# Two transformer blocks on one core: split scores four steps ahead, head turns three steps ahead, and the order of the second block's projections

## The chip, the cores and the metric

One core of one Trainium2 chip runs the whole program. The metric is the device time of one execution in microseconds (us). The engines are TensorE (PE; its weight loads are shown as PEld), VectorE (DVE), ScalarE (ACT), GpSimd (POOL) and SyncE (SP, which issues the loads of the weights).

## The reference

Input x is 512 tokens of 1024 columns. Two layers of a first block are followed by two layers of a second block. The first block has spatial gating, a latent attention of 8 heads (96 columns a head) and a gated linear attention, mixed by sigmoid gates. The change works mostly on the second block, of which one layer is:

```
h = rms_norm(x, norm_g); proj = h @ w_in          # 1024 -> aq ak av ag | bq bk bv bg | mq mg
qa, ka = rope(rms_norm(heads of aq)), rope(rms_norm(heads of ak))       # 6 heads of 64, causal
qb, kb = rope(rms_norm(heads of bq)), rope(rms_norm(heads of bk))       # 6 heads of 64, dilated
mkv = rms_norm(mem) @ w_mem_kv; qm, km = rms_norm(heads)                # 4 heads of 64, 256 memory rows
o = softmax(q @ k.T / 8 + mask) @ v                                     # for each head
x = x + concat(oa * silu(ag), ob * silu(bg), om * silu(mg)) @ w_out
```

All inputs and results are float32. The kernel computes a product of two float32 matrices with three passes of rounded parts: each operand is a high part (type float32r) and a low part (the rest), and the passes are high*high, high*low and low*high, summed in PSUM.

## The kernel before

**Matrix products of the projections.** `plan_groups` (L88) lists the groups of weight columns in the order in which they are used; in the second block mkv, aq, ak, av, bq, bk, bv, mq, ag, bg, mg, out. A group has 8 parts of 128 rows (a step in the ring). SP loads pieces of two parts into `raw`. For each part ACT writes the rounded `w_hi` (`round_weights`, L1036) and DVE writes the rest, `w_lo` (`residue`, L1361), both into a ring of four slots; ACT waits until the part four places back has been used. PE then runs the part's twelve (or nine) passes (`step`, L677, matmuls at L699). A `Splitter` on ACT and one on DVE keep three parts ahead of PE. `evict` and `evict_now` empty the four banks of a group.

**The order of each engine is written out by hand.** `alongside` (DVE) does the split of one part and then so many items of a generator (`per_step`), such as `head_norm` and `rotate`, in which each `yield` ends an item. `head_squares` on ACT makes the squares whose sums `head_norm` takes.

**Attention as a stream.** `Stream` makes units (a pair of heads g and a block i of 128 queries; a causal unit has i+1 key blocks, a memory unit two) and steps (at most two key blocks of a unit). In the second block there are 8 pairs, 32 units and 44 steps in a layer. Each engine walks the same steps. PE in step n: the events of `begin[n]`, a share of the remaining projections as filler (`fill`; bv, mq, ag, bg, mg and five parts of out), the product with v of the pair before (`values`, L795) in a pair's first step, and the transposes of the step's probabilities (`turn_probs`, L783). The events are `turn` (transposes of q and k of a pair of heads, L754), `scores` (L766) and, on DVE, `scale`. The chain of a unit is: scores on PE, mask and row maximum on DVE (L1522), Exp on ACT (L1091), reciprocal and scale on DVE (L1530, L1534), transposes on PE, copy on ACT (L1105), product with v.

**What sets the order before.** Scores of a unit stand two steps ahead of its first step. Probabilities have three buffers. The turn of a pair stands one to five steps ahead of its first scores. Scores of two heads are two float32 matmuls of 128 rows: `kT_2` holds each head's keys with zeros in the other head's half (POOL writes the zeros once), so DVE makes three copies for each turn (L1502, and L1506 twice). Scores and turns share the two PSUM banks `S_BANKS`. A score needs its bank read by whoever had it last. On ACT and DVE a step's `split_beside` moves the weight splits on: on ACT ahead of the step's other work, on DVE after `begin[n]` and ahead of `extra(n)`.

**Evictions.** DVE empties ak, bq, bv and mq; ACT empties aq, av, bk and the gates (with Silu).

## Time and profile before

| | |
|---|---|
| median of 3 runs | 1673.48 us (1673.45 to 1674.01) |
| the profiled execution's own time | 1672.92 us |
| span of its instructions | 1671.1 us |
| busy shares of the span | PE 96%, PEld 79%, DVE 59%, ACT 44%, POOL 3% |
| first layer of block 2, attention | about 1121 to 1321 us of the span |
| second layer of block 2, attention | about 1437 to 1640 us |

Busy time is the union of the instructions of an engine. A matmul's end is modelled, so successive passes overlap in the profile: what one costs PE is the distance from its start to the next start. "Idle" is the time in which nothing of the engine runs, and a releaser is the instruction that ended it. A float32 matmul is two records in the profile, a float32r pass one. "Granted clock" is the share of TensorE's full clock.

### The profile page before, as it was taken

To read this page: it belongs to the slowest core of one execution; us is meant where nothing else is said; L and a number is where in the kernel's file an instruction comes from. 1 tells how busy PE (TensorE), PEld (TensorE's weight loads), DVE (VectorE), ACT (ScalarE), POOL (GpSimd) and SP (SyncE) were. 2 spreads that over 40 slices of the span, in tenths; PEclk is the share of its full clock that TensorE was granted. 3 is DMA by queue.
4 is the path that set the end of the run, shared out by engine and by line. 5 is a ranking of instruction groups with operands and counts; after the bars stand their busy time and mean duration, and the time that the engine had idled before them with its cause. 6 is when DMAs were issued, how large, how long until landed. Compare 5 with 4: busy or idle time off the path is not lost.

```text
span 1671.1 us, 21692 instructions
## 1 busy us (share of the span) xinstructions
PE 1601.1 (96%) x8121; PEld 1317.0 (79%) x8121; DVE 993.0 (59%) x2214; ACT 730.1 (44%) x1503; POOL 48.1 (3%) x76
## 2 busy tenths in 40 slices
PE   6999999999999999999999999999989999998999
PEld 6887778788887887777788887998766789975677
DVE  4597655444344488756443445487876555688663
ACT  4444444333233443543433334435456554344662
POOL 0000001000001000001000001000000010000000
PEclk9999999999999999999999999999999999999999
DMA  7332122333333332112333232331112223211121
GB/s 221 88 88 75 51 64 64 101 89 89 102 98 95 93 90 76 51 51 77 88 89 101 89 126 82 104 86 54 57 29 73 91 87 95 79 51 42 35 76 63
DMA packets 80884, 136.24 MB, mean 82 GB/s; under 512 B 8190, under 2 KB 33420, under 8 KB 80780
## 3 DMA queue, kind: packets, MB, share of 16 engines
q1 hardware_dynamic: 77264, 129.48, 26.0%
q10 hardware_dynamic: 3516, 5.37, 1.0%
q8 instruction: 65, 1.06, 0.3%
q14 instruction: 39, 0.32, 0.1%
HBM read 132.74 MB, written 2.10 MB: 81 GB/s over the span
## 4 chain that ended last, share of the span: by engine, by line
PE 75%; DVE 17%; ACT 5%; issue 2%; DMA 0%; ACTq 0%; POOL 0%; DVEq 0%
PE gemm_bank L699 61%; PE aux_bank L766 4%; PE aux_bank L795 3%; DVE w_lo L1367 3%; PE aux_bank L783 3%; DVE rope L1466 2%; ACT w_hi L1044 1%; PE aux_bank L754 1%; DVE head_sums L1419 1%; DVE probs L1522 1%; ACT probs L1091 1%; DVE kT L1506 1%; DVE probs L1534 1%; PE aux_bank L671 1%; PE aux_bank L730 1%
## 5 line engine op out<-in xcount | busy, mean ns | idle before, releaser
L1044 ACT ACTIVATE w_hi<-raw 128x512 fp32r<-128x512 f32 (+3 forms) x524 | 305.6, 587 | 669.6 <-PE gemm_bank L699 668.2
L1367 DVE TENSOR_TENSOR w_lo<-raw,w_hi 128x512 fp32r<-128x512 f32 (+3 forms) x524 | 330.3, 636 | 442.6 <-ACT w_hi L1044 441.0
L699 PE MATMUL gemm_bank<-act_hi,w_hi 128*128 128x512 f32 x768 | 316.5, 412 | 7.9 <-DVE mq_flat L1407 3.8
L699 PE MATMUL gemm_bank<-act_hi,w_lo 128*128 128x512 f32 x768 | 300.4, 391 | 0.0
L699 PE MATMUL gemm_bank<-act_lo,w_hi 128*128 128x512 f32 x768 | 299.8, 390 | 0.0
L699 PE MATMUL gemm_bank<-w_hi,act_hi 128*128 128x384 f32 (+3 forms) x736 | 269.6, 366 | 6.1 <-DVE bq L1407 2.9
L699 PE MATMUL gemm_bank<-w_lo,act_hi 128*128 128x384 f32 (+3 forms) x736 | 257.6, 350 | 0.0
L699 PE MATMUL gemm_bank<-w_hi,act_lo 128*128 128x384 f32 (+3 forms) x736 | 257.4, 350 | 0.0
L699 PEld LDWEIGHTS gemm_bank<-act_hi,w_hi 128*128 128x128 f32 x768 | 144.7, 188 | 43.8 <-issue 11.2
L699 PEld LDWEIGHTS gemm_bank<-act_lo,w_hi 128*128 128x128 f32 x768 | 144.8, 189 | 31.8 <-issue 2.9
L699 PEld LDWEIGHTS gemm_bank<-act_hi,w_lo 128*128 128x128 f32 x768 | 144.4, 188 | 31.0
L699 PEld LDWEIGHTS gemm_bank<-w_hi,act_hi 128*128 128x128 f32 x736 | 139.4, 189 | 23.9 <-issue 9.7
L699 PEld LDWEIGHTS gemm_bank<-w_lo,act_hi 128*128 128x128 f32 x736 | 139.4, 189 | 11.3 <-issue 1.9
L699 PEld LDWEIGHTS gemm_bank<-w_hi,act_lo 128*128 128x128 f32 x736 | 139.1, 189 | 9.7
L766 PE MATMUL aux_bank<-kT,qT 128*128 128x256 f32 (+7 forms) x384 | 121.6, 435 | 5.9 <-DVE kT L1506 4.8
L1105 ACT ACTIVATE probsT<-aux_bank 128x256 f32<-128x256 f32 (+1 forms) x136 | 71.8, 528 | 114.3 <-PE aux_bank L783 113.5
L1091 ACT ACTIVATE probs<-probs,neg_max 128x128 f32<-128x128 f32 (+2 forms) x192 | 104.2, 544 | 35.6 <-DVE neg_max L1522 35.2
L783 PE MATMUL aux_bank<-ident,probs 128*128 128x128 f32 x464 | 75.7, 279 | 14.4 <-DVE probs L1534 14.2
L766 PEld LDWEIGHTS aux_bank<-kT,qT 128*128 128x128 f32 (+1 forms) x384 | 64.2, 193 | 27.5 <-DVE kT L1506 9.2
L783 PEld LDWEIGHTS aux_bank<-ident,probs 128*128 128x128 f32 x464 | 56.3, 141 | 37.0 <-DVE probs L1534 21.0
L699 PE MATMUL gemm_bank<-y_hi,w_hi 128*128 128x512 f32 x192 | 74.8, 390 | 0.3 <-ACT gate L1225 0.3
L699 PE MATMUL gemm_bank<-y_hi,w_lo 128*128 128x512 f32 x192 | 74.7, 389 | 0.0
(287 smaller groups left out, 2087.9 us busy)
## 6 DMA issues: line engine op xcount, KB each, us to landing
raw<-in_w_in SPq DMA_DIRECT2D x104, 512.0 KB, 3.6
raw<-in_w_in SPq DMA_DIRECT2D x64, 384.0 KB, 3.3
raw<-in_w_out SPq DMA_DIRECT2D x32, 512.0 KB, 3.7
raw<-in_w_branch SPq DMA_DIRECT2D x24, 512.0 KB, 3.7
raw<-in_w_mem_kv SPq DMA_DIRECT2D x8, 512.0 KB, 3.6
raw<-in_w_in SPq DMA_DIRECT2D x16, 256.0 KB, 2.8
raw<-in_w_in SPq DMA_DIRECT2D x8, 416.0 KB, 4.7
x<-in_x SPq DMA_DIRECT2D x4, 512.0 KB, 5.2
```

What stands on the lines that cost most here:

```text
L671: last = pe.transpose(bank[0:rows, t * P:(t + 1) * P], source(t, kk), ident[:, :])
L699: last = pe.matmul(o, a, c, start=begin and n == 0, stop=end and n == 2)
L730: last = pe.transpose(bank[:, t * P:(t + 1) * P], source[:, t, kk * P:(kk + 1) * P], ident[:, :])
L754: last = pe.transpose(bank[0:kind.rows, t * P:(t + 1) * P], of(h, t), ident[:, :])
L766: pe.matmul(bank[:, 0:n_keys * P], a.qT_of(g, x)[:, i * P:(i + 1) * P], a.kT_of(g, x)[:, 0:n_keys * P], start=True, stop=True).then_inc(fu ...
L783: last = pe.transpose(bank[:, c:c + P], probs[a.where][m % 3][:, x, j * P:(j + 1) * P], ident[:, :])
L795: last = pe.matmul(bank[x * HD:(x + 1) * HD, kind.first_i(j) * P:T], kind.v_of(a.head(g, x), j), a.probsT_of(g, x, j), start=(j == 0), sto ...
L1044: act.activation(w_hi[:, s % RING, 0:n], raw[:, p % RAW, kk % PIECE, 0:n], ACT.Copy)\
L1091: act.activation(rows, rows, ACT.Exp, bias=neg_max[:, c:c + 1], scale=-1.0, accum_out=row_sum[:, c:c + 1]).then_inc(probs_ready, 1)
L1105: act.activation(a.turned_to(m, j0, j1), bank[:, 0:2 * (j1 - j0) * P].rearrange("p (x j s) -> p x j s", x=2, s=P), ACT.Copy)\
L1367: dve.tensor_tensor(w_lo[:, s % RING, 0:n], raw[:, p % RAW, kk % PIECE, 0:n], w_hi[:, s % RING, 0:n].bitcast(F32), ALU.subtract).then_inc( ...
L1466: mark(dve.tensor_tensor(tmp[i][:, :, :, :], xx, t4, ALU.mult))
```

## The change

In the second block:

- The keys and queries turned by PE are split like weights: ACT writes the high parts (`turned_hi`), DVE, one step later, the low parts (event `low`). Scores are three float32r passes of 64 rows, head 0 in rows 0 to 63 and head 1 in rows 64 to 127, alternating (`scores_2`). The zeroed keys and their memset go.
- Scores stand up to four steps ahead, with four buffers of probabilities. `together` computes units 0 and 1 of a causal pair into one bank with one hand-over, and memory units two by two. Turns stand three steps ahead of their pair's first scores (two for pair 1, two for pair 7).
- av is projected last of the six, so that the first turn lies in av and not in bk; bq, bv and mq are emptied by ACT; the b heads' norm and rotation start beside av.
- On DVE a step's extra work comes ahead of its weight splits, and `rotate` yields after each instruction. In the first block DVE takes three items, not two, in each part of u and za.

The diff, cut to its core:

```diff
@@ -136,9 +136,9 @@
         two("mkv", 0, 2 * WE, NMEM // P, "w_mem_kv_2")
         two("aq", 0, WA)
         two("ak", WA, WA)
-        two("av", 2 * WA, WA)
         two("bq", 4 * WA, WB)
         two("bk", 4 * WA + WB, WB)
+        two("av", 2 * WA, WA)
         two("bv", 4 * WA + 2 * WB, WB)
         two("mq", 4 * WA + 4 * WB, WE)
         two("ag", 3 * WA, WA, WA // P)
...
@@ -526,11 +528,23 @@
                 self.steps += mine
             self.lead, self.middle = {}, {}
             self.begin = [[] for _ in self.steps]
+            self.turns, self.buffers = [], len(probs[self.where])
             for m, mine in enumerate(self.steps_of):
                 self.begin[mine[0]].insert(0, ("scale", m))
-                if mine[0] >= 2:
-                    self.begin[mine[0] - 2].append(("scores", m))
+                if mine[0] >= 2 and self.together(m):
+                    last = max(self.together(m)) - self.buffers
+                    free = self.steps_of[last][-1] + 1 if last >= 0 else 0
+                    self.begin[max(mine[0] - SCORES_LEAD[block], free, 0)].append(("scores", m))
             self.fill(fill, weight)
+        def together(self, m):
+            if self.block == 1:
+                return {m: 0}
+            kind, i = self.kind(m), m % NT
+            if kind.name == "memory":
+                return {} if i % 2 else {m: 0, m + 1: kind.n_keys(i) * P}
+            return {0: {m: 0, m + 1: P}, 1: {}}.get(i, {m: 0})
 
...
             self.begin[step].append(("turn", g, x))
+            if self.block == 2:
+                at = [event[0] for event in self.begin[step + 1]].index("scores") \
+                    if "scores" in [event[0] for event in self.begin[step + 1]] else len(self.begin[step + 1])
+                self.begin[step + 1].insert(at, ("low", g, x))
 
         def head(self, g, x):
...
                    DEPTH * UNITS_1 + l * UNITS_2, fill, lambda n: 1.3 if n < 13 else 0.9)
-        a.lead = {4: [("turn", 0, 0)], 5: [("scores", 0)], 6: [("scores", 1)]}
-        for g, (at_pair, step) in {1: (0, 1), 2: (0, 3), 3: (2, 1), 4: (2, 3), 5: (3, 3), 6: (4, 3), 7: (5, 3)}.items():
+        a.lead = {3: [("turn", 0, 0)], 4: [("low", 0, 0)], 5: [("scores", 0)]}
+        for g, (at_pair, step) in {1: (0, 0), 2: (0, 5), 3: (1, 5), 4: (2, 5), 5: (3, 5), 6: (4, 5), 7: (5, 4)}.items():
             a.turn_at(g, 0, a.first_step_of(at_pair) + step)
+        a.turns = list(range(len(a.pairs)))
         return a
 
...
 
+        def scores_2(a, m):
+            g, kind = m // NT, a.kind(m)
+            if m % NT == 0:
+                aux_wait_read(pe, a.key("q", g, 0))
+                aux_wait_read(pe, a.key("k", g, 0))
+            banks = [aux_open(a.key("S", m, x), S_BANKS[x]) for x in range(2)]
+            for mm, c in a.together(m).items():
+                i, keys = mm % NT, kind.n_keys(mm % NT) * P
+                for n, (qq, kk) in enumerate(((q_hi, k_hi), (q_lo, k_hi), (q_hi, k_lo))):
+                    for x in range(2):
+                        r = slice(x * HD, (x + 1) * HD)
+                        last = pe.matmul(banks[x][:, c:c + keys], qq[r, g % 2, i * P:(i + 1) * P],
+                                         kk[r, g % 2, 0:keys], start=n == 0, stop=n == 2)
+                        if n == 2 and mm == max(a.together(m)):
+                            last.then_inc(full_of(a.key("S", m, x)), 1)
         def begin(a, what, *of):
             if what == "turn":
                 turn(a, *of)
...
@@ -974,10 +1017,10 @@
 
         def block_2(l):
             gemm(gi_of(2, l, "aq"), "tokens", ready=part_ready((2, l, "x")))
-            for name in ("ak", "av", "bq"):
+            for name in ("ak", "bq", "bk"):
                 gemm(gi_of(2, l, name), "tokens")
             a = attention_2(l)
-            gemm_led(gi_of(2, l, "bk"), "tokens", a, lambda kk: None)
+            gemm_led(gi_of(2, l, "av"), "tokens", a, lambda kk: None)
             y_ready = lambda kk: pe.wait_ge(y2_lo_ready, KD * l + kk + 1)
             attention(a, y_ready)
...
                 wait_gemm_full(act, gi, b)
                 act.activation(dst(b), gemm_bank[b][:, 0:groups[gi].n], func).then_inc(gemm_read[b], 1)
 
+        def turned_hi(a, g):
+            for what, hi in (("q", q_hi), ("k", k_hi)):
+                bank = aux_wait_full(act, a.key(what, g, 0))
+                n = T if what == "q" else a.pairs[g][0].k_tiles * P
+                act.activation(hi[:, g % 2, 0:n], bank[:, 0:n], ACT.Copy).then_inc(turned_hi_ready, 1)
         def exponentials(a, m):
-            kind, i = a.kind(m), m % NT
-            keys = kind.n_keys(i) * P
-            for x in range(2):
-                c = a.column(m) + x
-                aux_wait_read(act, a.key("S", m, x))
-                rows = probs[a.where][m % 3][:, x, 0:keys]
-                act.activation(rows, rows, ACT.Exp, bias=neg_max[:, c:c + 1], scale=-1.0,
-                               accum_out=row_sum[:, c:c + 1]).then_inc(probs_ready, 1)
+            for mm in a.together(m):
+                for x in range(2):
...
             for n, (m, j0, j1) in enumerate(a.steps):
                 split_beside(split, a, n, evict_beside)
+                for event in a.begin[n] if a.block == 2 else ():
+                    if event[0] == "turn":
+                        turned_hi(a, event[1])
                 for event in a.begin[n] + a.middle.get(n, []):
                     if event[0] == "scores":
...
             for n, _ in enumerate(head_squares(kind_tiles("a"), sq_2)):
-                split.beside(gi_of(2, l, "av"), n // 2)
-            evict(gi_of(2, l, "av"), ACT.Copy, lambda b: flat_2("av")[:, b, :])
-            split.through(gi_of(2, l, "bq"))
-            a = attention_2(l)
-            gi = gi_of(2, l, "bk")
-            split.beside(gi, 5)
-            exponentials(a, 0)
-            split.beside(gi, 6)
-            exponentials(a, 1)
-            evict(gi, ACT.Copy, lambda b: flat_2("bk")[:, b, :])
+                split.beside(gi_of(2, l, "bq"), n // 2)
+            for name in ("bq", "bk"):
+                evict(gi_of(2, l, name), ACT.Copy, lambda b: flat_2(name)[:, b, :])
             wait_gemm_read(act, gi_of(2, l, "bq"))
             wait_gemm_read(act, gi_of(2, l, "bk"))
             b_squares = head_squares(kind_tiles("b"), sq_2)
+            a = attention_2(l)
+            gi = gi_of(2, l, "av")
+            for kk in range(KD):
+                for _ in range(2):
+                    next(b_squares, None)
+                split.beside(gi, kk)
+                if kk == 3:
+                    turned_hi(a, 0)
+                if kk == 6:
+                    exponentials(a, 0)
+            evict(gi, ACT.Copy, lambda b: flat_2("av")[:, b, :])
             m_squares = head_squares([mq_tok[:, t, :, :] for t in range(NT)]
...
             for i, xx in enumerate((x1, x2, x1, x2)):
                 t4 = table[:, i, :, :].unsqueeze(2).to_broadcast([P, NT, heads, half])
                 mark(dve.tensor_tensor(tmp[i][:, :, :, :], xx, t4, ALU.mult))
-                if i % 2:
-                    yield
+                yield
             settle()
             mark(dve.tensor_tensor(x1, tmp[0][:, :, :, :], tmp[1][:, :, :, :], ALU.subtract))
+            yield
             mark(dve.tensor_tensor(x2, tmp[2][:, :, :, :], tmp[3][:, :, :, :], ALU.add))
             yield
 
...
                 scaled(a, *of)
 
         def turned(a, g, x):
-            kind = a.pairs[g][0]
-            bank = aux_wait_full(dve, a.key("q", g, x))
-            dve.tensor_copy(a.qT_of(g, x), bank[0:kind.rows, :]).then_inc(read_of(a.key("q", g, x)), 1)
-            bank = aux_wait_full(dve, a.key("k", g, x))
-            for hh in range(kind.group):
-                r = slice(hh * kind.d, (hh + 1) * kind.d)
-                ins = dve.tensor_copy(a.kT_of(g, x + hh)[r, 0:kind.k_tiles * P], bank[r, 0:kind.k_tiles * P])
-                if hh == kind.group - 1:
-                    ins.then_inc(read_of(a.key("k", g, x)), 1)
-                else:
-                    mark(ins)
+            if a.block == 1:
+                bank = aux_wait_full(dve, a.key("q", g, x))
+                dve.tensor_copy(a.qT_of(g, x), bank[0:QK, :]).then_inc(read_of(a.key("q", g, x)), 1)
+                bank = aux_wait_full(dve, a.key("k", g, x))
+                dve.tensor_copy(a.kT_of(g, x), bank[0:QK, :]).then_inc(read_of(a.key("k", g, x)), 1)
+                return
+            for n, (what, hi, lo) in enumerate((("q", q_hi, q_lo), ("k", k_hi, k_lo))):
+                key = a.key(what, g, 0)
+                columns = T if what == "q" else a.pairs[g][0].k_tiles * P
+                dve.wait_ge(turned_hi_ready, 2 * a.turn_count(g) - 1 + n)
+                dve.tensor_tensor(lo[:, g % 2, 0:columns], aux_bank[aux_place[key][0]][:, 0:columns],
+                                  hi[:, g % 2, 0:columns].bitcast(F32), ALU.subtract).then_inc(read_of(key), 1)
 
         def scores(a, m):
 
-            kind, i = a.kind(m), m % NT
-            keys = kind.n_keys(i) * P
-            if m >= 3:
-                aux_wait_full(dve, a.key("T", a.steps_of[m - 3][-1]))
+            kind, units = a.kind(m), a.together(m)
+            if max(units) >= a.buffers:
+                aux_wait_full(dve, a.key("T", a.steps_of[max(units) - a.buffers][-1]))
             for x in range(2):
-                c = a.column(m) + x
                 key = a.key("S", m, x)
                 bank = aux_wait_full(dve, key)
-                dve.tensor_tensor_reduce(out=probs[a.where][m % 3][:, x, 0:keys], in0=bank[:, 0:keys],
-                                         in1=kind.mask(i), scale=-kind.scale, scalar=3.0e38, op0=ALU.add, op1=ALU.min,
-                                         accum_out=neg_max[:, c:c + 1]).then_inc(read_of(key), 1)
+                for mm, b in units.items():
+                    c, keys = a.column(mm) + x, kind.n_keys(mm % NT) * P
+                    ins = dve.tensor_tensor_reduce(out=probs[a.where][mm % a.buffers][:, x, 0:keys],
+                                                   in0=bank[:, b:b + keys], in1=kind.mask(mm % NT), scale=-kind.scale,
+                                                   scalar=3.0e38, op0=ALU.add, op1=ALU.min,
+                                                   accum_out=neg_max[:, c:c + 1])
+                    if mm == max(units):
+                        ins.then_inc(read_of(key), 1)
+                    else:
+                        mark(ins)
 
...
                 for event in a.begin[n] + a.middle.get(n, []):
                     if drain and event[0] == "turn":
                         drain(event[1])
-                    begin(a, *event)
+                    else:
+                        begin(a, *event)
+                extra(n)
                 split_beside(split, a, n, evict_beside)
-                extra(n)
                 g = m // NT
                 if g and n == a.first_step_of(g):
                     evicted_out(a, g - 1, evict_out)
...
 
             a = attention_1(l)
             work = prepare()
-            alongside(work, [gi_of(1, l, n) for n in ("u", "za")], 2, at_end, False)
+            alongside(work, [gi_of(1, l, n) for n in ("u", "za")], 3, at_end, False)
 
             def sum_out(g):
...
+            alongside(a_heads, [gi_of(2, l, n) for n in ("bq", "bk")], 2)
             for kk in range(KD):
                 for event in a.lead.get(kk, []):
-                    begin(a, *event)
-                split.beside(gi_of(2, l, "bk"), kk)
+                    if event[0] != "turn":
+                        begin(a, *event)
+                for _ in range(2):
+                    next(b_heads, None)
+                split.beside(gi_of(2, l, "av"), kk)
 
             def drain(g):
                 for _ in b_heads if g == FIRST_B else m_heads if g == FIRST_M else ():
```

## Rows read from the trace of the kernel before

**Rows 1.** The page: busy time by engine, and the chain by engine.

```profile
PE 1601.1 (96%) x8121; PEld 1317.0 (79%) x8121; DVE 993.0 (59%) x2214; ACT 730.1 (44%) x1503; POOL 48.1 (3%) x76
...
PE 75%; DVE 17%; ACT 5%; issue 2%; DMA 0%; ACTq 0%; POOL 0%; DVEq 0%
```

**Rows 2.** Busy time in both attentions of block 2: PE, PEld, DVE, ACT, POOL, clock.

```profile
1121.30:1321.60 200.30, 187.34 (x1005) 146.08 (x1005) 139.01 (x409) 106.57 (x264) 0.00 (x0) 0.99 0.18 56
1436.80:1640.50 203.70, 188.89 (x1005) 147.19 (x1005) 139.38 (x409) 105.48 (x263) 0.00 (x0) 0.98 0.18 55
```

**Rows 3.** PE's waits, 1121 to 1321.5; last row 1436.7 to 1640.5: total, times, longest.

```profile
PE aux_bank L783 <- DVE probs L1534: 6.0, 5, 2.0
PE aux_bank L766 <- DVE kT L1506: 2.4, 5, 0.8
PE aux_bank L795 <- ACT probsT L1105: 1.5, 1, 1.5
PE gemm_bank L699 <- DVE bq L1407: 1.4, 1, 1.4
PE gemm_bank L699 <- DVE mq_flat L1407: 1.1, 1, 1.1
PE gemm_bank L699 <- DVE bv L1407: 0.8, 1, 0.8
PE aux_bank L766 <- DVE qT L1502: 0.5, 1, 0.5
...
PE gemm_bank L699 <- DVE mq_flat L1407: 2.7, 1, 2.7
```

**Rows 4.** The chain in order of time: start, us, what, count.

```profile
245.09 19.27 PE gemm_bank L699 x84
...
1052.75 31.22 PE gemm_bank L699 x180
...
1176.25 1.72 PE aux_bank L766 x4
```

**Rows 5.** Timeline of PE, 256-column passes after scores: start, duration.

```profile
1177.92 0.28 PE L699 MATMUL gemm_bank<-w_lo,act_hi 128*128 128x256 f32 x1
1178.04 0.28 PE L699 MATMUL gemm_bank<-w_hi,act_lo 128*128 128x256 f32 x1
```

**Rows 6.** Timeline of PE in the linear attention of block 1.

```profile
264.19 1.03 PE L671 MATMUL aux_bank<-ident,qk_c 128*128 128x128 f32 x8
265.16 2.27 PE L925 MATMUL aux_bank<-qk_c,kt_dn 64*128 64x128 f32 x32
267.36 1.13 PE L940 MATMUL aux_bank<-vc,ks_tok 64*64 64x128 f32 x16
```

**Rows 7.** DVE by line and shape, 1045 to 1361: busy us, mean ns.

```profile
L1367 DVE TENSOR_TENSOR w_lo<-raw,w_hi 128x512 fp32r<-128x512 f32 x24 | 16.1, 689 | 14.6 <-ACT w_hi L1044 14.6
...
L1506 DVE COPY kT<-aux_bank 64x512 f32<-64x512 f32 x12 | 8.2, 684 | 0.2
...
L1522 DVE CUSTOM_DVE_ANT_0 probs<-aux_bank,mask_causal 128x384 f32<-128x384 f32 x6 | 3.2, 553 | 1.0 <-PE aux_bank L766 1.0
...
L1534 DVE TENSOR_SCALAR probs<-probs,row_inv 128x128 f32<-128x128 f32 x12 | 2.9, 284 | 0.2
```

**Rows 8.** ACT by line and shape, the same stretch.

```profile
L1105 ACT ACTIVATE probsT<-aux_bank 128x512 f32<-128x512 f32 x32 | 18.8, 588 | 16.8 <-PE aux_bank L783 16.5
L1044 ACT ACTIVATE w_hi<-raw 128x512 fp32r<-128x512 f32 x24 | 14.4, 625 | 9.1 <-PE gemm_bank L699 9.1
```

**Rows 9.** PE by stretch, before and after its longest wait: busy, granted clock.

```profile
1185.00:1188.00 3.00, 1.25 (x11) 1.00 0.03 10
1188.00:1192.00 4.00, 3.91 (x16) 0.57 0.30 98
```

**Rows 10.** PE's waits in block 1's first layer, 60 to 165.

```profile
PE aux_bank L754 <- DVEq L1476: 1.6, 1, 1.6
PE gemm_bank L699 <- DVE w_lo L1367: 1.0, 2, 0.7
```

62 lines of the change are left out of this document (32 added, 30 removed).

## The prediction

> **What bounds the kernel now.** I read the page first: PE is busy for 96% of the span and holds 75% of the chain [rows 1], so time comes mainly from less PE work or fewer PE waits. The stretches of the two attentions of block 2 come next [rows 2]: 200.3 and 203.7 us, with PE busy for 187 and 189, DVE 139, ACT 106. No engine but PE is near its bound over the whole of a stretch, so what PE waits for there is order and latency. Third, PE's waits in that stretch [rows 3]: 14.1 us of idle time in 16 waits, most of it for scaled probabilities (6.0), turned keys and queries (2.4 + 0.5), and evictions by DVE (bq 1.4, mq 1.1, bv 0.8). The second layer has the same rows except mq, 2.7; with it 16.0 us. A wait costs a little more than its idle time, because a modelled end covers part of the next start: from the starts in the timeline I take 0.2 us more each. That makes 17.3 + 19.2 = 36.5 us of waits in both layers that this change could touch.
>
> **PE's work in the scores.** Before: four records of 512 columns (both heads) take 1.72 us [rows 4], so a block of 128 keys for both heads costs 0.43. A causal pair has 10 blocks, 4.30 us; a memory pair 8, 3.44. After: a float32r pass has a start-to-start distance of 19.27/84 = 0.229 us at 512 columns and 31.22/180 = 0.173 at 384 [rows 4], and 0.12 at 256 [rows 5]. The trace has no float32r pass of 128 columns and none on half the rows. For the half rows the nearest rows are those of the linear attention [rows 6]: 32 records of 64 rows, alternating halves and banks, take 2.20 us (265.16 to 267.36), where 8 records of 128 rows take 0.97, 0.12 each. At 0.12 each one after the other they would take 3.9. So both halves work at the same time; two side by side cost 0.11 to 0.14. I take 0.11 for a pair of 128-column passes, and what 16 x 0.11 = 1.8 leaves of 2.2, 0.2 for each of its two batches, as the price of changing over to half rows. A causal pair then costs 3 x (0.11 + 0.12 + 0.173 + 0.229) = 1.90 plus three batches x 0.2, 2.5 us: 1.8 less. A memory pair costs 4 x 3 x 0.12 = 1.44 plus two batches, 1.84: 1.6 less. Six and two pairs give 14.0 us a layer, **28.0 in both**. Bounds: with no price for changing over, 22 batches x 0.2 x 2 = 9 more is gained; if the passes of the two heads add up, 4.4 and 3.28 us a pair, nothing is gained (28 worse). If a 128-column pass costs what float32 does (0.21), 3 x 0.1 x 6 x 2 = 3.6 comes back.
>
> The Trainium skill speaks against the half rows: "TensorEngine Tiling (Array Packing)", Key Properties, says that changing the tiling mode drains TensorE. The row gives 0.2 us for a batch, on entry. If leaving cost as much again, 44 x 0.2 = 9 us would come back and the sum below would be 1648.
>
> **Waits that go.** Scores four steps ahead, with the mask, Exp and scale of a unit two steps further from its transposes, cover the waits for probabilities. ACT empties bq, bv and mq bank by bank (0.49 us for 384 columns by the rows of other evictions) while PE works on; PE's next group then finds bank 0 free. The waits for probabilities, bq, bv and mq go: 9.3 us idle in layer one, 10.9 in two, with 9 x 0.2 each 23.8 together. The cover is DVE's: beside av it has 16 items of b_heads, eight weight parts, a low pair and the first masks, some 17 us against 18.3 of PE; in steps 0 to 5 some 24 against 22. So DVE is the later one there, and I leave 1.5 us a layer for it. The 2.05 us of three copies a turn (0.69 + 2 x 0.68) [rows 7] become two low parts on DVE (1.38) and two high parts on ACT (0.59 each, from a copy out of PSUM) [rows 8]; ACT gains some 16 us a layer on 106 and is no bound.
>
> **Waits that come.** Turn and scores share two banks. Turns 2 to 6 are transposed in a pair's last step n, the low part is made at the start of n+1, and scores of another unit follow there at once; they need both banks read. ACT comes to the high part only after its weight split, which waits for PE's last part but one. From that moment: w_hi 0.63 [rows 8], w_lo 0.69 [rows 7], scale of a 128-key unit 0.16 + 2 x 0.28, low q and low k 0.69 each, and semaphores 0.3, about 3.4 us; PE has 0.9 to 1.8 us of filler and transposes left (step 11 has ACT's eviction of mq in the way as well, 1.5 us). By the filler of each step I get waits of 2.0, 2.0, 0.4, 2.2 and 2.5 us: 9.1 a layer, in place of 2.9 idle and 1.2 of restarts before. In step 0 scores of unit 2, scores of unit 3 and turn 1 follow each other through the same two banks. Behind each stand PE's latency of 0.35, two masks (2 x 0.55 at 384 columns, and 2 x 0.69 at 512, which is what every DVE operation of 512 columns takes) [rows 7] and 0.3 of semaphores, less the batch's own 0.5 to 0.7: 1.5 and 1.9, 3.4 us that did not exist. What stands behind these waits is PE's filler, no more.
>
> Sum for both layers: before 36.5; after 2 x (9.1 + 3.4 + 1.5) = 28.0, plus 4.6 for the waits of `values` and of the gate bg, which stay: 32.6. **3.9 us less.**
>
> **Block 1.** PE waits 1.6 us for the heads at its first turn and 1.0 for weight parts [rows 10]; the second layer has the same two. DVE's timeline shows hardly a gap from 97 us to that turn, at 139. At three items a part, the heads are done before u is multiplied by za (2.4 us), so the 1.6 goes and the waits for weight parts stay or grow a little. I take 1.5 a layer, 3.0; bounds 2 us worse (parts late) and 5 better.
>
> **Hidden or nothing.** POOL's memset, the order of av (its product comes 12 us later), a fourth probability buffer: PE has waits on none of them in [rows 3]. SP's loads follow the same ring; av's only change place. I take 0 us, with one either way.
>
> **The sum** is made against the profiled execution's 1672.9 us, 0.6 under the median of the runs: 1672.9 - 28.0 - 3.9 - 3.0 = 1638.0, in terms of the median **1638.6**.
>
> **Rivals.**
>
> *Heads one after the other.* The passes of the two halves add up: nothing of the 28.0 is gained, 1667. Against it are the 2.20 us of [rows 6]; for it, that these are float32 records and not float32r. 7%.
>
> *Few new waits.* The turns' waits stay at what they are before (4.1 a layer, not 9.1) and step 0's halve, since ACT reaches the high parts earlier than I reckon: 2 x (5.0 + 1.7) = 13.4 less, 1625. For it: step 18's is only 0.4 by the same working. 25%.
>
> *The clock.* After a wait of 1.84 us the granted clock is 0.57 over 4 us, part full and part at 1.2 GHz instead of 2.4, which costs 4 x 0.43 = 1.7 us [rows 9]; each layer has one such stretch. If all seven new waits are followed by one, 14 x 1.7 = 24 less the 3.4 of before: 1659. Against it: the longest wait of that layer, 2.0 us [rows 3], is followed by none. 9%. (The Trainium skill, "TensorE: Matmul & The Clock Gate", part 1, says idle time sends the clock to half; the row agrees, 0.57 after 1.84 us.)
>
> *Weight parts late, slower than before.* DVE now takes its scores, which wait for PE's, and two items before a step's weight split. Once DVE is more than the ring's three parts behind (about 6 us of PE's filler), PE waits for w_lo in every step. From 35/88 = 0.4 us a step on, over 88 steps, the gain is gone; at 0.5 it is 1683. For it: DVE's share in steps 0 to 18 is near PE's. Against it: PE's waits for w_lo in the attentions before are nil in [rows 3] though DVE was as busy. 6%.
>
> **Chances.** The forecast has 53%. The range that should hold 8 in 10 goes from 1614 (few new waits and no changeover price) to 1662 (clock, or most of the half-row gain lost). About 0.2%, 3.3 us, is what a measurement of this kernel can tell from no change. Faster by more: 0.91; within: 0.03; slower: 0.06.
>
> **What would show it.** Right: scores of 512 keys, both heads, take about 0.7 us of PE instead of 1.72, with starts of the two halves a few ns apart; no PE wait for probabilities, bq, bv, mq; a new PE wait for k_lo of about 9 us a layer in five places, and for the masks in step 0. Wrong: equal distances between all six passes of a unit (heads in turn), PE waits for w_lo above 2 us a layer, clock stretches after each k_lo wait, or k_lo waits under 4 us a layer.

## The result and the profile after

The changed kernel takes 1676.9 us where the kernel before takes 1673.6 in the same comparison (20 runs each): ratio 1.0022, 95% interval 1.0014 to 1.0029. It is 3.4 us slower by the medians, 0.2%, and not 35 us faster. One of the six runs of a_two below took 2207.3 us at a granted clock of 0.68, in a slow state: without it the median is 1663.1, with it the 1663.9 that the expectations name. The profiled execution has a span of 1673.4 us, 2.3 more than the one before. Its page answers to [rows 1]:

```profile
PE 1589.0 (95%) x8249; PEld 1307.8 (78%) x8249; DVE 969.8 (58%) x2174; ACT 750.1 (45%) x1559; POOL 46.4 (3%) x75
...
PE 83%; DVE 10%; ACT 5%; issue 2%; DMA 0%; ACTq 0%; POOL 0%; DVEq 0%
```

PE is busy for 12 us less in a span that is 2 us longer, so some of the saving is there, and more idle time (14 us) stands against it. The page does not say where.

The first view to read is one row for each stage, from the transposes of x_n of a block to those of the next. Columns: stretch, length, then busy time with the number of instructions of PE, PEld, DVE, ACT and POOL, granted clock, DMA share, GB/s. Before:

```profile
12.00:523.40 511.40, 501.10 (x2457) 410.23 (x2457) 286.57 (x570) 207.34 (x386) 16.45 (x20) 1.00 0.30 87
523.40:1043.60 520.20, 507.87 (x2497) 413.97 (x2497) 292.27 (x572) 214.82 (x401) 22.37 (x29) 1.00 0.29 86
1043.60:1359.20 315.60, 299.32 (x1606) 248.83 (x1605) 211.44 (x547) 158.17 (x371) 5.56 (x14) 0.99 0.24 71
1359.20:1668.00 308.80, 292.37 (x1565) 243.80 (x1563) 200.66 (x527) 142.90 (x335) 0.00 (x0) 0.99 0.22 66
```

After:

```profile
12.50:530.80 518.30, 503.38 (x2456) 410.11 (x2457) 286.54 (x570) 206.61 (x385) 16.45 (x20) 0.99 0.30 86
530.80:1058.90 528.10, 513.48 (x2497) 417.56 (x2498) 292.60 (x572) 214.89 (x401) 20.55 (x28) 0.98 0.29 85
1058.90:1370.10 311.20, 290.46 (x1670) 243.73 (x1669) 199.68 (x527) 168.25 (x399) 5.56 (x14) 0.98 0.24 72
1370.10:1670.20 300.10, 281.25 (x1629) 236.18 (x1627) 188.82 (x506) 153.21 (x363) 0.00 (x0) 0.98 0.23 68
```

Two things cancel. Block 1, the first two rows, is longer by 6.9 + 7.9 = 14.8 us, though PE's work in it is the same. Block 2 is shorter by 4.4 + 8.7 = 13.1 us, well short of the 31.9 forecast for it. The granted clock is lower in all four rows. Before, the trace has 4 stretches at half clock (1.2 GHz instead of 2.4) of 3.4 us each, one of them in block 1. After, it has 11 of about 3.4 us and two of 6.8, five of them in block 1 (23.9 us), seven in block 2 (23.9 us) and one at the very end.

PE's waits in both attentions of block 2, first layer and second (total, times, longest), are the rows that answer to [rows 3]:

```profile
PE aux_bank L807 <- DVE k_lo L1571: 8.6, 5, 2.0
PE aux_bank L826 <- DVE probs L1601: 5.1, 4, 2.4
PE aux_bank L826 <- ACT probsT L1160: 1.7, 2, 1.2
PE aux_bank L807 <- DVE neg_max L1584: 1.6, 1, 1.6
PE gemm_bank L721 <- ACT bgT L1380: 1.1, 1, 1.1
PE aux_bank L776 <- DVE neg_max L1584: 0.8, 1, 0.8
...
PE aux_bank L807 <- DVE k_lo L1571: 7.4, 4, 2.0
PE aux_bank L826 <- DVE probs L1601: 5.4, 4, 2.4
PE aux_bank L826 <- ACT probsT L1160: 2.8, 3, 1.2
```

The waits for bq, bv and mq are gone and those for k_lo have come, as forecast. The waits for scaled probabilities (L826 for probs) have stayed: 5.1 and 5.4 us, 6.0 before. The idle time is 18.9 and 18.7 us in place of 14.1 and 16.0.

In block 1, PE's waits from 60 to 165 us, to be held against [rows 10]:

```profile
PE gemm_bank L721 <- DVE w_lo L1428: 7.6, 4, 3.6
PE gemm_bank L721 <- DVE c_lo L1455: 0.9, 1, 0.9
```

The wait for the heads at the first turn (1.6) is gone, as intended, and weight parts cost 7.6 in its place. DVE's timeline shows why (start, duration, what, count; idle time before it and its releaser in brackets):

```profile
80.40 0.68 DVE L1428 TENSOR_TENSOR w_lo<-raw,w_hi 128x512 fp32r<-128x512 f32 x1
81.00 2.46 DVE L1715 BATCH_NORM_STATS2 stats<-vn 128x6 f32<-128x512 f32 x4
...
86.34 0.68 DVE L1428 TENSOR_TENSOR w_lo<-raw,w_hi 128x512 fp32r<-128x512 f32 x1
87.96 1.81 DVE L1480 TENSOR_REDUCE head_sums<-sq 128x8 f32<-128x768 f32 x2 [0.93 <-ACT sq L1107]
90.68 0.95 DVE L1480 TENSOR_REDUCE head_sums<-sq 128x8 f32<-128x768 f32 x1 [0.91 <-ACT sq L1107]
91.55 0.68 DVE L1428 TENSOR_TENSOR w_lo<-raw,w_hi 128x512 fp32r<-128x512 f32 x1
...
95.12 0.68 DVE L1428 TENSOR_TENSOR w_lo<-raw,w_hi 128x512 fp32r<-128x512 f32 x1
...
101.70 0.69 DVE L1428 TENSOR_TENSOR w_lo<-raw,w_hi 128x512 fp32r<-128x512 f32 x1
```

These five weight parts start 5.3 us apart on average (21.3 / 4), where PE works one off in 12 x 0.229 = 2.7. The items between them are the dear ones: statistics of 2.5 us, sums of 768 columns of 0.95 each that also wait for ACT's squares, and a chain of twelve small steps for the roots. With three of them a part, DVE uses up its lead over PE, and PE has to wait. Three of its four waits fall here (0.4, 0.5 and the first line below). The fourth comes later in the same way: the weight parts at 111.53 and 117.68 stand 6.2 us apart, with two products of 2.5 us between them.

```profile
102.44 0.79 PE L721 MATMUL gemm_bank<-act_hi,w_hi 128*128 128x512 f32 x1 [3.57 <-DVE w_lo L1428]
...
118.42 0.50 PE L721 MATMUL gemm_bank<-act_hi,w_hi 128*128 128x512 f32 x1 [3.13 <-DVE w_lo L1428]
```

The scores themselves overlap as forecast, but take longer: 512 keys of both heads 1.09 us, where the sign of being right was 0.7. Timeline of PE, one unit of 384 keys, both heads; `64*128` with x2 is one pass of each head:

```profile
1173.15 0.38 PE L826 MATMUL aux_bank<-ident,probs 128*128 128x128 f32 x2
1173.46 0.44 PE L807 MATMUL aux_bank<-k_hi,q_hi 64*128 64x384 f32 x2
1173.74 0.34 PE L807 MATMUL aux_bank<-k_hi,q_lo 64*128 64x384 f32 x2
1173.91 0.33 PE L807 MATMUL aux_bank<-k_lo,q_hi 64*128 64x384 f32 x2
1174.18 0.44 PE L721 MATMUL gemm_bank<-w_hi,act_hi 128*128 128x384 f32 x1
1174.46 0.34 PE L721 MATMUL gemm_bank<-w_lo,act_hi 128*128 128x384 f32 x1
```

The recorded starts of the two heads are 3 ns apart: both work at once. But something stands at either end of the batch. The two transposes end their share at 1173.37 (1173.15 + 2 x 0.11), the second gemm pass starts at 1174.46, and the first one's share is 0.17: the batch took 1174.29 - 1173.37 = 0.92 us, and its passes are 3 x 0.173 = 0.52. The other 0.40 stands half before the first and second pass of the batch and half before the first and second pass behind it, on full rows.

### The profile page after: what moved, and what is told of

Same layout as the page of the kernel before. It is cut to its first block, busy times and chain, and to the rows that moved or that the text cites. A ratio compares the mean times of both kernels' runs of the same rounds, so it can differ in the third digit from the quotient of the medians.

```text
span 1673.4 us, 21983 instructions
## 1 busy us (share of the span) xinstructions
PE 1589.0 (95%) x8249; PEld 1307.8 (78%) x8249; DVE 969.8 (58%) x2174; ACT 750.1 (45%) x1559; POOL 46.4 (3%) x75
## 4 chain that ended last, share of the span: by engine, by line
PE 83%; DVE 10%; ACT 5%; issue 2%; DMA 0%; ACTq 0%; POOL 0%; DVEq 0%
PE gemm_bank L721 69%; PE aux_bank L838 3%; PE aux_bank L826 3%; PE aux_bank L807 2%; PE aux_bank L791 2%; DVE w_lo L1428 2%; PE aux_bank L776 1%; ACT probs L1143 1%; ACT w_hi L1087 1%; DVE probs L1601 1%; DVE probs L1584 1%; DVE head_sums L1480 1%; PE aux_bank L693 1%; PE aux_bank L752 1%; PE aux_bank L997 0%
## 5 line engine op out<-in xcount | busy, mean ns | idle before, releaser
L721 PE MATMUL gemm_bank<-act_lo,w_hi 128*128 128x512 f32 x768 | 304.2, 396 | 0.0
L721 PE MATMUL gemm_bank<-act_hi,w_lo 128*128 128x512 f32 x768 | 304.1, 396 | 0.0
L826 PE MATMUL aux_bank<-ident,probs 128*128 128x128 f32 x464 | 75.2, 278 | 15.5 <-DVE probs L1601 10.6
L826 PEld LDWEIGHTS aux_bank<-ident,probs 128*128 128x128 f32 x464 | 55.9, 141 | 38.6 <-DVE probs L1601 16.5
L721 PE MATMUL gemm_bank<-y_lo,w_hi 128*128 128x512 f32 x192 | 74.7, 389 | 0.0
L1601 DVE TENSOR_SCALAR probs<-probs,row_inv 128x128 f32<-128x128 f32 (+2 forms) x192 | 64.5, 378 | 3.4
```

Of the source, the lines that this page charges most:

```text
L721: last = pe.matmul(o, a, c, start=begin and n == 0, stop=end and n == 2)
L826: last = pe.transpose(bank[:, c:c + P], probs[a.where][m % a.buffers][:, x, j * P:(j + 1) * P], ident[:, :])
L1601: ins = dve.tensor_scalar(rows, rows, row_inv[:, c + x:c + x + 1], None, ALU.mult)
```

## Experiments

Each was timed in rounds with the kernel before, and the ratio is to that one. "Stages" are the four of the first view.

| run | edit | us | ratio, 95% |
|---|---|---|---|
| change | | 1676.9 | 1.0022 [1.0014, 1.0029] |
| a_two | two items a part in block 1 | 1663.1 | 0.9935 [0.9919, 0.9950] |
| b_three | before, with three items | 1692.4 | 1.0108 [1.0092, 1.0123] |
| c_low | a_two, low parts in the turn's step | 1648.1 | 0.9843 [0.9828, 0.9858] |
| d_mlater | a_two, memory items a step later | 1659.4 | 0.9904 [0.9886, 0.9921] |
| e_both | c_low and d_mlater | 1636.9 | 0.9783 [0.9771, 0.9796] |
| f_split_first | a_two, extra items behind the split | 1677.9 | 1.0026 [1.0017, 1.0036] |
| g_heads_in_turn | a_two, passes of one head, then the other | 1664.4 | 0.9949 [0.9937, 0.9961] |
| h_lead_two | a_two, scores two steps ahead | 1665.4 | 0.9950 [0.9936, 0.9964] |
| i_before_halves | before, float32 scores on half rows | 1662.1 | 0.9932 [0.9919, 0.9944] |
| j_plain | e_both, float32 scores on half rows | 1635.0 | 0.9769 [0.9755, 0.9782] |
| l_uza | e_both, u times za later | 1629.3 | 0.9738 [0.9725, 0.9751] |
| m_single | l_uza, one unit a batch | 1635.8 | 0.9768 [0.9755, 0.9782] |
| k_plain_uza | j_plain and l_uza | 1628.6 | 0.9729 [0.9716, 0.9742] |

**a_two and b_three: the number of items.**

```
-            alongside(work, [gi_of(1, l, n) for n in ("u", "za")], 3, at_end, False)
+            alongside(work, [gi_of(1, l, n) for n in ("u", "za")], 2, at_end, False)
```

> The changed kernel with one edit taken back: in the first block DVE takes two items, not three, in each part of u and za. Theory (three items a part starve PE of weight parts): PE's waits for w_lo before the first turn fall from 7.6 and 6.8 us in the two layers to about 1.5 each, the half-clock stretches of 3.4 us there (2 and 3) go, and the time falls by about 14 us, to 1663. Rival (the first block lost its time through the single-instruction items of rotate, or through extra work ahead of the splits in its attention): the waits for w_lo stay near 7 us and the time stays at 1675 to 1677.

> The kernel before with that edit alone: three items a part in u and za. Theory: it alone costs what the first block lost, 12 to 15 us, 1686 to 1688, with 6 to 8 us of PE waits for w_lo in each layer. Rival (it needs the finer items of rotate to do harm): 1672 to 1676.

a_two: 14 us less than the change, with stages of 513.2, 521.3, 311.3 and 300.0: what the stages give, 11.9, is all from block 1. PE's waits there, with two items:

```profile
PE aux_bank L776 <- DVEq L1537: 3.8, 1, 3.8
PE gemm_bank L721 <- DVE c_lo L1455: 0.9, 1, 0.9
PE gemm_bank L721 <- DVE w_lo L1428: 0.3, 1, 0.3
```

The wait at the first turn, 1.6 before the change, is 3.8 here, and block 1 is still 2.9 us longer than before. In the timeline the four products of a rotation now fill two weight parts instead of one, since `rotate` yields after each instruction, and so the heads are done later.

b_three is the same edit put into the kernel before: 18 us more, and block 1 longer by 19.2 (521.5 and 529.3). PE's wait for weight parts from 60 to 165 us:

```profile
PE gemm_bank L699 <- DVE w_lo L1367: 7.2, 5, 3.5
```

So the third item alone makes the loss in block 1, and does so without the rest of the change. The rest of the change is worth 1 - 0.9935, 11 us.

**c_low: the low parts.** ACT makes the high parts ahead of its weight split, and DVE the low parts in the turn's own step instead of the next.

```
             for n, (m, j0, j1) in enumerate(a.steps):
-                split_beside(split, a, n, evict_beside)
                 for event in a.begin[n] if a.block == 2 else ():
                     if event[0] == "turn":
                         turned_hi(a, event[1])
+                split_beside(split, a, n, evict_beside)
...
-                    else:
+                    elif event[0] != "low":
                         begin(a, *event)
                 extra(n)
+                for event in a.begin[n] if a.block == 2 else ():
+                    if event[0] == "turn":
+                        turned(a, *event[1:])
                 split_beside(split, a, n, evict_beside)
```

> As a_two, and in the second block ACT writes the high parts of a turn ahead of its weight split, and DVE the low parts in the step of the turn, after the extra work and ahead of its split, not at the start of the next step. Theory (PE waits for k_lo because both engines reach the parts only after a weight split that itself waits for PE): the waits for k_lo fall from 8.6 us in five places to under 1.5 a layer, some of the half-clock stretches behind them go, and the time falls by 15 to 22 us against a_two, to about 1644. Rival (DVE is the bound there, and what it does earlier it lacks later): the wait turns up as a wait for probabilities or masks, and the time is within 6 us of a_two.

15 us less than a_two. The waits for k_lo fall from 8.6 and 7.4 to 0.7 and 1.5, those for probabilities stay (5.2 and 5.3). The stages of block 2 are 16.9 us shorter: their idle time falls from 39.6 to 27.2, and their half-clock stretches go from 7 to 4, 1.7 us each. Block 1, which the edit does not touch, is 2.7 us longer, with four such stretches for three.

**d_mlater: the memory heads' sums.** After step n's transposes ACT makes squares for the memory heads, and DVE adds them up within its extra items. In the changed kernel these stand ahead of the weight split and the next scale, and wait for the squares. DVE's waits from 1205 to 1234 us in the changed kernel:

```profile
DVE head_sums L1480 <- ACT sq L1107: 9.0, 3, 4.9
```

Two of the three in its timeline:

```profile
1217.08 0.74 DVE L1480 TENSOR_REDUCE head_sums<-sq 128x4 f32<-128x256 f32 x2 [4.93 <-ACT sq L1107]
1217.74 0.55 DVE L1428 TENSOR_TENSOR w_lo<-raw,w_hi 128x384 fp32r<-128x384 f32 x1
1218.21 0.68 DVE L2028 COPY ya_T<-aux_bank 128x512 f32<-128x512 f32 x1
1218.81 0.15 DVE L1597 RECIPROCAL row_inv<-row_sum 128x2 f32<-128x2 f32 x1
1219.00 0.62 DVE L1601 TENSOR_SCALAR probs<-probs,row_inv 128x256 f32<-128x256 f32 x2
1221.30 0.74 DVE L1480 TENSOR_REDUCE head_sums<-sq 128x4 f32<-128x256 f32 x2 [1.69 <-ACT sq L1107]
```

PE had been waiting for that scale and came to its transposes at once behind it:

```profile
1219.67 0.66 PE L826 MATMUL aux_bank<-ident,probs 128*128 128x128 f32 x4 [1.95 <-DVE probs L1601]
```

```
-                for work in [b_heads] + [m_heads] * (n > n_m):
+                for work in [b_heads] + [m_heads] * (n > n_m + 1):
```

> As a_two, and DVE starts the norm of the memory heads one step later (step 13, not 12). Theory (DVE's extra work now stands ahead of its split and of the next step's scale, and its sums wait for squares that ACT makes only after PE's transposes of the same step: 9.0 us of DVE idle in three waits between 1205 and 1234): those waits go, PE's waits for probabilities fall from 5.1 us to about 1.5 a layer, and the time falls by 7 to 11 us against a_two, to about 1654. Rival (these waits come from DVE's load in steps 12 to 18): no change against a_two, within 2 us.

The waits for probabilities fall from 5.1 and 5.4 to 1.1 and 1.1, as expected, so their cause is shown. The time falls by 3.7 us only, where 7 to 11 were expected: the waits for k_lo rise to 10.3 in both layers, and the first layer (311.0) is no shorter at all, with 20.5 us at half clock in place of 13.7.

**e_both.**

> The changed kernel with two heads' items a weight part in block 1, the low parts of a turn made in the turn's own step, and the memory heads' items one step later. Theory (the waits for k_lo and those for scaled probabilities are separate and add): from the run with early low parts (1648.1) the probability waits fall from 5.2 and 5.3 us to about 1.1 a layer, 8 to 9 us less, k_lo stays under 2 a layer: 1639.5. Rival 1 (clock): what the waits give is taken by half-clock stretches that fall elsewhere, as in the first layer of the run with later items: 1644. Rival 2 (the same delay seen twice): with DVE's later items the low parts come late again, k_lo back at 5 or more a layer: 1648.

26 us less than a_two, where the two edits by themselves gave 15 and 3.7. In the stages of block 2 it is 25.6, and by themselves 16.9 and 6.7, so they add there, and a little more. One part of the theory fails: the waits for k_lo are 3.2 in both layers, not under 2, and above the 0.7 and 1.5 of c_low. The later items still push the low parts back, by less than rival 2 had it. The waits for probabilities are 1.1 and 1.1.

**f_split_first: the order on DVE.**

```
+                split_beside(split, a, n, evict_beside)
                 extra(n)
-                split_beside(split, a, n, evict_beside)
```

> The changed kernel with two items a part, and DVE's extra items of a step behind the step's weight part again, as before the change. Theory (the sums of the memory heads wait on DVE for ACT's squares, and scales and weight parts stand behind them): the weight part no longer stands behind the sums but the next step's scale still does: probability waits 5.1 to about 3 a layer, 4 us less in all than with two items: 1660. Rival (the place of the items in the step is what makes the waits): both waits of 2 us vanish, 8 less: 1656. Rival (nothing): 1664, waits as before. Block 1 stays within 2 us.

Both the theory and its rivals fall: it is 15 us slower than a_two. Waits for k_lo go from 8.6 and 7.4 to 11.0 and 9.8, those for probabilities from 5.1 and 5.4 to 6.5 and 7.1, and block 2 has 37.5 us at half clock in place of 23.9. By the order of the program the extra items, sums included, then stand right ahead of the next step's scale and low parts; that this is the cause was not tested by itself. The extra items hurt in either place, and "ahead of the weight part" is the better one; with the rest of the change, that part of it is a gain.

**g_heads_in_turn: do the halves need each other as neighbours?** The x loop is put outside the three passes.

> The changed kernel with two items a part; the three passes of a unit's scores are issued for one head and then for the other, not alternately. Theory (passes on different halves of the rows run side by side only when they are neighbours in the order): of six passes two neighbours still overlap, the others add up: a causal pair 1.58 us more, a memory pair about 1.2, 6 x 1.6 + 2 x 1.2 = 12 us a layer less the overlap across units: 19 us more than 1663.9, 1683. Rival (no overlap worth having, all six add up and did so already): 1664. Rival (nothing overlaps when in turn): 28 more, 1692. In the timeline the starts of one head's passes are a full pass apart.

No difference beyond the intervals. One rival had the time, but for a reason that the trace denies: there is an overlap. In this kernel the program says q_hi, q_lo, k_lo of head 0, then the same of head 1; the timeline shows the pairs of both heads side by side all the same, with starts 10 to 41 ns apart:

```profile
1171.47 0.50 PE L807 MATMUL aux_bank<-k_hi,q_hi 64*128 64x512 f32 x2 [1.95 <-DVE k_lo L1571]
1171.78 0.43 PE L807 MATMUL aux_bank<-k_hi,q_lo 64*128 64x512 f32 x2
1172.01 0.58 PE L807 MATMUL aux_bank<-k_lo,q_hi 64*128 64x512 f32 x2
```

Each half takes its own passes in order and does not wait for the other's.

**h_lead_two: is the lead of four steps worth anything?** `SCORES_LEAD` of block 2 is 2.

> The changed kernel with two items a part and the scores of block 2 two steps ahead as before the change, not four. Theory (the lead of four hides the way from the mask to the scaled probability; the waits of 2 us come from the memory sums and are there with either lead): waits for probabilities rise from 5.1 to about 9 a layer, waits for k_lo fall from 8.6 and 7.4 to about 4, since the scores stand further behind the turn: 1663, within 4 of 1663.9. Rival (the lead brings the gain): k_lo waits stay, probabilities 6 a layer worse: 1676. Rival (the lead is harmful): waits for probabilities stay at 5, k_lo falls to 3: 1654.

The intervals overlap; waits for probabilities 4.5 and 4.9, for k_lo 9.1 and 8.0. The time follows the theory, but not its working: neither wait moved by more than 0.6. The lead brings nothing in this kernel, where PE waits for a scale that is late behind the sums (d_mlater). Whether it brings something once those waits are gone, as in e_both, was not run.

**i_before_halves: the saving of the halves by itself.** In the kernel before, one kT without zeros, and

```
-                pe.matmul(bank[:, 0:n_keys * P], a.qT_of(g, x)[:, i * P:(i + 1) * P],
-                          a.kT_of(g, x)[:, 0:n_keys * P], start=True, stop=True).then_inc(full_of(key), 1)
+                r = slice(x * HD, (x + 1) * HD) if kind.group == 2 else slice(0, kind.rows)
+                pe.matmul(bank[:, 0:n_keys * P], a.qT_of(g, x)[r, i * P:(i + 1) * P],
+                          a.kT_of(g, x)[r, 0:n_keys * P], start=True, stop=True).then_inc(full_of(key), 1)
```

> The kernel before with one thing changed: the scores of block 2 are plain float32 products on half the rows, one head on each half, from one kT without zeros; everything else, order and leads too, as before. Theory (the halves work side by side whatever their order, also in float32): a causal pair 4.30 becomes 2.15 plus 0.2 for each of four batches, a memory pair 3.44 becomes 1.72 plus 0.8, 6 x 1.35 + 2 x 0.92 = 9.9 us a layer, 20 in both; one copy of 0.69 less a turn, 2 us of kT waits less in both layers: 1652. Rival (the overlap belongs to float32r): nothing from PE, 1672. Rival (the saving of the halves is taken back by waits for probabilities, since PE comes to them earlier): 1660.

11.4 us, not 21. Float32 passes do run side by side, so that rival is out. The rival at 1660 has nearly the time, but not the cause: the waits for probabilities are 5.8 in both layers, where they were 6.0 and 6.2. The timeline of a 512-key batch, kernel before and then this one:

```profile
1175.65 0.60 PE L783 MATMUL aux_bank<-ident,probs 128*128 128x128 f32 x4
1176.09 1.88 PE L766 MATMUL aux_bank<-kT,qT 128*128 128x512 f32 x4
1177.40 0.69 PE L699 MATMUL gemm_bank<-w_hi,act_hi 128*128 128x256 f32 x1
```

```profile
1174.62 0.60 PE L784 MATMUL aux_bank<-ident,probs 128*128 128x128 f32 x4
1175.15 1.13 PE L767 MATMUL aux_bank<-kT,qT 64*128 64x512 f32 x4
1176.21 0.39 PE L699 MATMUL gemm_bank<-w_hi,act_hi 128*128 128x256 f32 x1
1176.43 0.28 PE L699 MATMUL gemm_bank<-w_lo,act_hi 128*128 128x256 f32 x1
```

Before, the second gemm pass starts at 1177.92 [rows 5], and less one pass of 0.12 the batch ends at 1177.80: 1.72 us after the transposes. On half rows it is from 1175.06 to 1176.31, 1.25 us, where half of 1.72 is 0.86. The same reckoning gives 0.62, 0.83 and 1.04 at 128, 256 and 384 columns: always 0.40 above half (0.22, 0.43 and 0.65). A layer then saves 32.9 - 29.1 = 3.8 us, 7.6 in both; PE's waits give another 3.3 (26.8 in place of 30.1). That is 10.9 of the 11.4.

**j_plain: three float32r passes or one float32 pass.** q and k are copied by DVE alone, and ACT makes no high parts.

> The kernel with two items, early low parts and later memory items, but with plain float32 scores on the halves in place of three float32r passes: no high and low parts of q and k, two copies a turn on DVE, none on ACT. Theory (one float32 pass costs 0.86 at 512 columns where three float32r passes cost 0.69, 2 us a layer more; the k_lo waits of 3.2 a layer go, since DVE needs no ACT): 1636.9 + 4 - 6 = 1635, within 4 of 1636.9. Rival (the three passes are worth more than that, as in the width of the change itself): 1645. Rival (ACT's high parts held up its weight parts too): 1629.

The time is the theory's, 1635.0, but by luck: the waits that were to go did not. Batches are 1.06 to 1.27 us in place of 0.92 to 1.17, and the waits for k_lo of 3.2 become waits for kT of 3.1 a layer, so it was DVE's order that made those, not ACT; what became less is a wait for bgT (1.8 to 1.1) and for mq_flat (1.0 to nothing). In block 2 there are also two half-clock stretches fewer (one for three). Dearer passes against fewer waits and stretches: the split of q and k into parts is worth nothing that can be measured here.

**l_uza: work of DVE ahead of the first turn of block 1.**

```
-            alongside(work, [gi_of(1, l, n) for n in ("u", "za")], 2, at_end, False)
+            alongside(work, [gi_of(1, l, n) for n in ("u", "za")], 2, None, False)
...
                 split.beside(gi_of(1, l, "zb"), kk)
+                if kk == 5:
+                    at_end(gi_of(1, l, "za"))
```

> The kernel with two items, early low parts and later memory items, and in block 1 u times za moved from the end of za to behind the first turn beside zb. Theory (DVE has no gap for 45 us before the first turn of block 1 and the wait of 3.8 us there is for its heads, so every us of other work moved behind it comes off the wait): 2.49 us less a layer, 5 in both: 1632. The wait for DVEq at the turn 3.8 becomes 1.3. Rival (the product then stands ahead of a weight part or of the sums and makes a new wait there): 1637.

The wait at the turn is 1.4 (3.8 before the edit), as expected, and the time 7.5 us less, not 5. The idle time of block 1 is 5.4 less, and the half-clock stretches behind that wait (at 140 and 652 us in e_both) are gone too; one new stretch has come at 524 us.

**m_single and k_plain_uza.** `together(m)` returns `{m: 0}` in m_single, so each layer has 32 units in batches of their own, and the scores and Exp of unit 1 get their own place beside av.

> The kernel with u times za moved (1629.3), in which each unit's scores stand alone: 32 batches a layer in place of 21, same passes, same columns, same order otherwise. Theory (each batch on half rows costs 0.40 us beside its passes, about half going in and half coming out, as the starts around a batch show): 11 x 0.40 x 2 = 8.8 us more, 1638. Rival (only the way in costs, 0.2, as the prediction had it): 1633.7. Rival (a batch costs nothing by itself, the 0.4 are waits of the masks): 1629.

> The two edits that were best by themselves put together: plain float32 scores on the halves (1635.0) and u times za behind the first turn (7.5 less than 1636.9). Theory (they touch different stretches and add): 1627.5. Rival (the float32 passes cost 2 us a layer more PE time than float32r, and their gain was in waits that the other has no more): 1631.

m_single is 6.5 us slower than l_uza (5.0 by the ratios). A batch of 128 and 256 columns took 1.09 us; alone they take 0.68 and 0.75. Two of 256 took 1.11; alone 0.75 each. So an extra batch costs 0.34 to 0.39 us, 6 x 0.34 + 4 x 0.39 = 3.6 a layer, 7.2 in both, and the stages of block 2 are 5.9 us longer. There were 22 batches a layer before the edit, not the 21 of the expectation, so 10 more and not 11: at 0.40 each that makes 8.0. The price is one of each batch, in and out; "only the way in" would be 4.0, and the ratios alone would not exclude it, but the rows do. k_plain_uza is the fastest of all, 45 us faster than the kernel before, though not by more than its interval than l_uza.

## Why the prediction was wrong

- **PE's work in the scores: size off.** Six pairs of 4.3 and two of 3.5 were 32.9 us a layer before, as reckoned. After, batches of 1.09, 0.92 and 1.15 make 3.16 a causal pair, and two of 1.11 a memory pair: 6 x 3.16 + 2 x 2.22 = 23.4. The saving is 9.5 a layer, **19.0 in both and not 28.0**. The step that failed is "I take ... 0.2 for each of its two batches": it read the way in and left out the way out. [rows 6] could not show that one: behind the 32 records come more passes on 64 rows. The prediction had the other end in hand, in the sentence on the Trainium skill, "TensorEngine Tiling (Array Packing)", Key Properties, whose drain at a change of mode it priced at 9 us. The trace agrees with that rule: 0.40 us around each batch. But that all of it is the drain isn't shown: in [rows 6] the second batch too begins dearer (the starts around its first passes are 0.22 and 0.18 us apart, the others 0.11), though the passes right before it are on 64 rows as well. The rival "heads one after other" is out.
- **Waits that go: half right.** Those for bq, bv and mq went, 3.3 us in the first layer and 4.9 in the second. Those for probabilities stayed at 10.5 us of 12.2. The step that failed is "cover the waits for probabilities": it counted DVE's items in a step as work of a known length and did not ask what each of them waits for. The sums wait for squares that ACT makes after the transposes of the same step, so neither lead, four or two, reaches them (d_mlater, h_lead_two).
- **Waits that come: right in place and in size.** k_lo 8.6 and 7.4 in five and four places against 9.1 (in the first layer 1.9, 1.5, 1.2, 2.0 and 1.9 for 2.0, 2.0, 0.4, 2.2 and 2.5); neg_max 2.4 and 2.0 against 3.4; the rival "few new waits" is out. With the part above the waits add 7.5 us of idle time where the sum had 3.9 less.
- **The clock: a rival that partly came.** Stretches at half clock in block 2 go from 3 to 7, 4 x 1.7 = 6.8 us, against 20 forecast by that rival at 9%, and nothing by the sum. In block 1 they cost some 9 us more: half their length, with PE's idle time left out, is 10.7 us against 1.7.
- **Block 1: wrong sign, and the largest error.** Forecast 3.0 less, measured 14.8 more: 6.9 us more idle time and about 9 of clock. The step that failed is "the waits for weight parts stay or grow a little". It rests on DVE's timeline from 97 us on, and gives no length to the items. But the lead is used up between 80 and 102 us, and again by 118, where one item is up to 2.5 us or waits for ACT. Taken back (a_two) and put in alone (b_three), the third item gives -11.9 and +19.2 us in block 1. The rival "weight parts late" had this mechanism (lead of three parts, then a wait a part), but in block 2's attentions, where there are no waits for w_lo at all.
- **Small slips.** The sum counts nine restarts of 0.2 for eight waits a layer (0.4 us in both). Not every DVE operation of 512 columns takes 0.69: the scale takes 0.48; the masks, which the sum uses, do take 0.69.

Block 2 in sum: -19.0 + 7.5 + 6.8 = -4.7, and -13.1 was measured. Some 8 us more came than these rows hold. Of it 3 to 4 can be seen in the ten batches of scores before in which PE waited for kT: besides the recorded idle time they take longer than the others (2.19 us where others take 1.72, 0.88 where others take 0.45), and hardly so after. The rest stays open, and no run was made on it. Added up, the errors are 9.0 (scores), 11.4 (waits), 6.8 (clock) and 17.8 us (block 1), less the 8.4 of block 2 just named, 36.6; by the spans the forecast is off by 37.2.

## What to carry to other kernels

Before an engine's work between two deadlines is made denser, list the items one by one with their lengths and with what each waits for: an average over the stretch hid that three dear items follow each other where the lead is smallest, and that a reduction stood for another engine's later work. A wait of PE can cost itself plus a half-clock stretch behind it, here 1.7 us a time: in the changed kernel such a stretch followed 10 of the 14 waits of 1.8 us or more. And a small batch on half the rows carries a fixed price that is paid twice, so fewer and larger batches are part of the gain.

## What the runs showed of the hardware

- Going to passes on 64 rows and back costs 0.40 us of PE's time for each batch, nearly the same for float32 and float32r (0.35 to 0.40) and for 128 to 512 columns (0.62, 0.83, 1.04 and 1.25 us for float32, both heads, where half of the old time is 0.22, 0.43, 0.65 and 0.86; for float32r 0.68, 0.75, 0.92 and 1.09, where three passes are 0.33, 0.36, 0.52 and 0.69).
- Passes on the two halves of the rows run side by side even when the program issues three of one half before the first of the other: in the timeline they start 10 to 41 ns apart, and the kernel takes 1664.4 us against 1663.1.
- A single float32 pass on half rows of 512 columns (0.86 us for both heads) costs 0.17 more than three float32r passes (0.69), and spares the parts.
- Removing waits shortened a stage by more than its idle time in three runs: block 2 by 16.9 us for 12.3 (c_low), block 1 by 7.5 for 5.4 (l_uza) and by 11.9 for 6.2 (a_two), and each time it had fewer stretches at half clock (7 to 4, 2 to 1, 5 to 3).
